# Modulation products of later layers as row sums on VectorE inside the MLPs, in place of TensorE pieces inside the mixers

## What is computed

```
# block 1, layer l (two vectors: c and c_ctx)
mx = split(silu(c)     @ w_ada[l] + b_ada[l], 6)        # w_ada[l]: 1024 x 6144
mc = split(silu(c_ctx) @ w_ada[l] + b_ada[l], 6)
hx = rmsnorm(x) * g * (1 + mx[1]) + mx[0]               # and the same for ctx
x  = x + mx[2] * rmsnorm(token_mixers(hx, ...))         # mLSTM, Fourier, convolution
hx = rmsnorm(x) * g * (1 + mx[4]) + mx[3]
x  = x + mx[5] * rmsnorm(square(relu(hx @ w1)) @ w2)    # the MLP, 1024 -> 4096 -> 1024
# block 2, layer l (one vector: c_2)
shift, scale, gate = split(silu(c_2) @ ada_w_2[l] + ada_b_2[l], 3)   # 1024 x 3072
```

## Time and profile before

| | us |
|---|---|
| median of 3 runs (3286.33 to 3298.46) | 3289.57 |
| span of the profiled execution | 3296.2 |
| TensorE busy in it | 3061.9 (93%) |
| VectorE busy | 1369.8 (42%) |
| ScalarE busy | 1076.6 (33%) |
| GpSimd busy | 1119.3 (34%) |
| L997, 1152 records of 72 ada pieces | 101.5 |

### The profile page before, as it was taken

How to read it: one execution, slowest core, us unless ns; L and a number is a source line. 1 busy time by engine, 2 the same in 40 slices (tenths; PEclk the granted TensorE clock), 3 DMA queues, 4 the chain that set the end, 5 groups by cost and what they waited for, 6 DMA issues and landing times.

```text
span 3296.2 us, 42947 instructions
## 1 busy us (share of the span) xinstructions
PE 3061.9 (93%) x16748; PEld 2466.0 (75%) x16748; DVE 1369.8 (42%) x2601; ACT 1076.6 (33%) x1995; POOL 1119.3 (34%) x862
## 2 busy tenths in 40 slices
PE   7998879999999988978999999999889999998898
PEld 4687658888888866856788876777678767776786
DVE  4683432512122158242531125644482255434822
ACT  3223432323222242243333332233433322334332
POOL 1121104133233422203344442342355523332555
PEclk9999869899999979988899989999999899999999
DMA  5232252121111112333222222121112222121121
GB/s 205 90 141 84 100 195 77 45 64 63 60 65 64 65 59 78 112 113 109 100 96 96 91 84 77 64 69 67 58 58 77 85 71 70 65 65 64 58 77 64
DMA packets 77720, 275.49 MB, mean 84 GB/s; under 512 B 8512, under 2 KB 10304, under 8 KB 77392
## 3 DMA queue, kind: packets, MB, share of 16 engines
q1 hardware_dynamic: 75824, 268.91, 24.0%
q10 hardware_dynamic: 1696, 3.84, 0.3%
HBM read 270.62 MB, written 2.10 MB: 83 GB/s over the span
## 4 chain that ended last, share of the span: by engine, by line
PE 82%; DVE 11%; ACT 3%; issue 2%; POOL 1%; DMA 1%; SPq 0%; DVEq 0%; ACTq 0%; POOLq 0%
PE pb L1054 19%; PE pb L1056 18%; PE pb L1055 18%; PE pb L1165 2%; PE pb L997 2%; PE pb L1076 2%; PE pb L1078 2%; PE pb L1077 2%; PE pb L1093 1%; DVE AR L1717 1%; PE pb L1094 1%; PE pb L1095 1%; PE pb L1123 1%; PE pb L1173 1%; PE pb L1299 1%
## 5 line engine op out<-in xcount | busy, mean ns | idle before, releaser
L2622 POOL TENSOR_TENSOR RGR<-RG,WHI 128x512 fp32r<-128x512 f32 x708 | 933.9, 1328 | 1746.3 <-ACT WHI L2210 1745.5
L2210 ACT ACTIVATE WHI<-RG 128x512 fp32r<-128x512 f32 x708 | 436.9, 624 | 711.4 <-PE pb L1056 600.5
L1054 PE MATMUL pb<-HI,WHI 128*128 128x512 f32 (+1 forms) x880 | 374.5, 426 | 10.5 <-DVE LO L1645 4.9
L1056 PE MATMUL pb<-LO,WHI 128*128 128x512 f32 (+1 forms) x880 | 351.3, 399 | 0.0
L1055 PE MATMUL pb<-HI,RGR 128*128 128x512 f32 (+1 forms) x880 | 350.7, 398 | 0.0
L1054 PE MATMUL pb<-HR,WHI 128*128 128x512 f32 (+1 forms) x768 | 276.8, 360 | 8.1 <-DVE HR L1645 5.6
L1056 PE MATMUL pb<-HR,WHI 128*128 128x512 f32 (+1 forms) x768 | 276.9, 361 | 0.0
L1055 PE MATMUL pb<-HR,RGR 128*128 128x512 f32 (+1 forms) x768 | 276.6, 360 | 0.0
L1056 PE MATMUL pb<-HIDR,WHI 128*128 128x512 f32 (+1 forms) x768 | 274.7, 358 | 0.0
L1055 PE MATMUL pb<-HIDR,RGR 128*128 128x512 f32 (+1 forms) x768 | 274.2, 357 | 0.0
L1054 PE MATMUL pb<-HIDR,WHI 128*128 128x512 f32 (+1 forms) x768 | 273.3, 356 | 0.0
(11 more groups left out here) (407 smaller groups left out, 5665.1 us busy)
## 6 DMA issues: line engine op xcount, KB each, us to landing
RG<-in_W_dram SPq DMA_DIRECT2D x504, 512.0 KB, 3.5
XCX<-in_xT_dram ACTq DMA_DIRECT2D x4, 512.0 KB, 12.2
out_dram<-XCX SPq DMA_DIRECT2D x8, 256.0 KB, 2.1
CS<-in_CST_dram ACTq DMA_DIRECT2D x1, 1027.0 KB, 4.8
XCC<-in_ctxT_dram SPq DMA_DIRECT2D x4, 256.0 KB, 13.9
CS<-in_CST_dram SPq DMA_DIRECT2D x1, 523.0 KB, 4.7
RG<-in_W_dram SPq DMA_DIRECT2D x2, 256.0 KB, 2.9
RG<-in_W_dram SPq DMA_DIRECT2D x2, 128.0 KB, 2.6
```

The costliest lines, as they stand in the source:

```text
L1054: e.matmul(out, hi[:, k, :], xh, start=k == order[0], stop=False)
L1056: i = e.matmul(out, hi[:, k, :], xl, start=False, stop=k == order[7])
L2210: e.activation(WHI[:, u % 2, h * n:h * n + n], RG[:, s % RING, h * n:h * n + n], ACT.Copy).then_inc(*up("weightsA", (u, h)))
L2622: e.tensor_tensor(RGR[:, s % RING, sl], RG[:, s % RING, sl], WHI[:, u % 2, sl].bitcast(F32), SUB).then_inc(*up("weightsG", (u, h)))
```

## The change

In the layer-0 mixer only the first 12 ada pieces stay (output channels 16 to 39 of w_ada[0], in units of 128), in the layer-1 mixer none of its 18. The other 84 units of 128 channels are computed as "columns": the slab now holds the transposed weights of 128 output channels, one channel to a partition, with the 1024 inputs along the row. VectorE multiplies it elementwise by silu(c), spread over all partitions, and sums along the row into `MODS`; for w_ada twice, for c and c_ctx. `spread` loads the spread vectors on ScalarE's DMA queue after w_out, `spreadSilu` applies Silu, `offsets` adds the biases after the MLP. In layer 0's MLP one column follows every task from the fifth to the 52nd, in layer 1's from the fifth to the 40th; the slab of a column enters the ring between two weight slabs, and the next slab but five waits for VectorE to have summed it.

```diff
+    def next_column(self):
+        if self.loaded and (len(self.loaded) > 1 or not self.sums):
+            self.step("column", self.loaded.pop(0))
+        if self.sums:
+            self.column(*self.sums.pop(0))
...
     def filling(self, us):
...
+        elif self.credit >= self.period and (self.sums or self.loaded):
+            self.credit = 0.0
+            self.next_column()
...
     if l == 0:
-        o.fill(8.5, (0, range(16, 48, 2), "w_ada", 0), (1, range(0, 40, 2), "w_ada", 1))
-    else:
-        o.fill(24.0, (2, range(0, 24, 2), "ada_w_2", 0), (3, range(8, 20, 2), "ada_w_2", 1))
+        o.fill(8.5, (0, range(16, 40, 2), "w_ada", 0))
...
+    o.step("spread", l)
...
+    if l == 0:
+        o.columns(8.0, (0, range(40, 48), "w_ada", 0), (1, range(0, 40), "w_ada", 1))
+    else:
+        o.columns(5.0, (2, range(0, 24), "ada_w_2", 0), (3, range(8, 20), "ada_w_2", 1))
+    o.step("spreadSilu", l)
     o.products(jobs, (0, 1, 2, 3), 2)
     o.flush()
+    o.columned()
...
             if i >= RING:
-                e.wait_ge(*at("matmuls", o.slabs[i - RING]["last"]))
+                older = o.slabs[i - RING]["last"]
+                e.wait_ge(*at("columnsV" if o.pieces[older]["kind"] == "column" else "matmuls", older))
...
+        def column(n):
+            p = o.pieces[n]
+            s, i = p["slabs"][0], p["i"]
+            w = RG[:, s % RING, :]
+            e.wait_ge(*at(f"slab{s % RING}", s))
+            e.wait_ge(*at("spreadA", min(i, 2)))
+            if i < 2:
+                if ("product", i) in seen:
+                    e.wait_ge(*now("columnsV"))
+                seen.add(("product", i))
+                e.scalar_tensor_tensor(out=PRODUCT, in0=w, scalar=1.0, in1=SPREAD[0][:, 0, :], op0=MUL, op1=MUL,
+                                       accum_out=MODS[i][:, p["j"], 0:1]).then_inc(*up("columnsV"))
+                e.wait_ge(*now("columnsV"))
+                e.scalar_tensor_tensor(out=w, in0=w, scalar=1.0, in1=SPREAD[0][:, 1, :], op0=MUL, op1=MUL,
+                                       accum_out=MODS[i][:, p["j"], 1:2]).then_inc(*up("columnsV", n))
+            else:
+                w4 = w.rearrange("p (a b) -> p a b", a=4)
+                e.scalar_tensor_tensor(out=w4, in0=w4, scalar=1.0, in1=SPREAD[1], op0=MUL, op1=MUL,
+                                       accum_out=MODS[i][:, p["j"], 0:1]).then_inc(*up("columnsV", n))
```

More of the change, by code:

```diff
@@ L157, in __init__ @@
         self.fills, self.soon, self.laid, self.held = [], [], [], []
+        self.sums, self.loaded = [], []
         self.credit, self.period = 0.0, 7.0
@@ L219, in ada, with column, columns, columned @@
         self.soon.append(n)
+    def column(self, i, j, name, l):
+        n = self.piece("column", [self.slab(name + ":T", l, 0, 8, j * 128, 128)], [], [], i=i, j=j, how="column")
+        self.last["column", i] = n
+        self.loaded.append(n)
+    def columns(self, period, *what):
+        self.period, self.credit = period, 0.0
+        for i, js, name, l in what:
+            self.sums += [(i, j, name, l) for j in js]
+    def next_column(self):
[3 more added lines that the diff above has]
+            self.column(*self.sums.pop(0))
+    def columned(self):
+        while self.sums or self.loaded:
+            self.next_column()
     def hold(self, i, j, name, l):
@@ L418, in place @@
                 first.setdefault(self.pieces[what[1]].get("unit"), i)
+            if what[0] == "column":
+                taken[what[1]] = i
             if what[0] == "ev":
@@ L606, in first_layer @@
     o.filled()
-    o.step("gains", l, (1, 2, 3))
+    o.step("gains", l, (1, 2) if l == 0 else (1, 2, 3))
     tag = f"o{l}a"
@@ L623, in first_layer @@
         tab = o.begin([("table", i) for i in range(7)], 12.0)
+    if l == 0:
[3 more added lines that the diff above has]
+    o.step("spreadSilu", l)
     o.products(jobs, (0, 1, 2, 3), 2)
     o.flush()
+    o.columned()
+    if l == 0:
+        o.step("offsets", 0, 40, 48)
+        o.step("offsets", 1, 0, 40)
+        o.step("gains", 0, (3,))
+    else:
+        o.step("offsets", 2, 0, 24)
+        o.step("offsets", 3, 8, 20)
     if tab:
@@ L1577, in post, with offsets @@
                 e.tensor_tensor(d, d, raw, ADD).then_inc(*up("evacV", ("roped", n)))
+        def column(n):
[13 more added lines that the diff above has]
+                                       accum_out=MODS[i][:, p["j"], 1:2]).then_inc(*up("columnsV", n))
+            else:
+                w4 = w.rearrange("p (a b) -> p a b", a=4)
+                e.scalar_tensor_tensor(out=w4, in0=w4, scalar=1.0, in1=SPREAD[1], op0=MUL, op1=MUL,
+                                       accum_out=MODS[i][:, p["j"], 0:1]).then_inc(*up("columnsV", n))
+        def offsets(i, j0, j1):
+            ns = 2 if i < 2 else 1
+            bias = vec(*(("b_ada", i) if i < 2 else ("ada_b_2", i - 2)))
+            mod = MODS[i][:, j0:j1, 0:ns]
+            e.wait_ge(*now("columnsV"))
+            e.tensor_tensor(mod, mod, bias[:, j0:j1].unsqueeze(2).to_broadcast([128, j1 - j0, ns]), ADD).then_inc(*up("columnsV", ("all", i, j0)))
         def xsum(k):
@@ L1598, in gains @@
         def gains(l, which):
-            e.wait_ge(*at("evacV", o.last["ada", l, 0 if which == (0,) else 2]))
+            if which == (3,):
+                e.wait_ge(*at("columnsV", ("all", 0, 40)))
+            else:
+                if which == (0,) and l:
+                    e.wait_ge(*at("columnsV", ("all", 1, 0)))
+                else:
+                    e.wait_ge(*at("evacV", o.last["ada", l, 0 if which == (0,) else 2]))
             e.wait_ge(*now("normV"))
@@ L1606, in gains2 @@
         def gains2(l, i):
-            e.wait_ge(*at("evacV", o.last["ada", 2 + l, i]))
+            if l == 0:
+                e.wait_ge(*at("columnsV", ("all", 2, 0)))
+            else:
+                e.wait_ge(*at("columnsV", ("all", 3, 8)))
+                e.wait_ge(*at("evacV", o.last["ada", 3, i]))
             e.wait_ge(*now("normV"))
@@ L2210, in split, with spread, spreadSilu @@
             e.activation(WHI[:, u % 2, h * n:h * n + n], RG[:, s % RING, h * n:h * n + n], ACT.Copy).then_inc(*up("weightsA", (u, h)))
+        def spread(l):
+            e.wait_ge(*at("matmuls", o.last["out", l, "evacV", None]))
+            if l == 0:
+                e.wait_ge(*at("normG", ("heads lo", 0, CHUNKS[1][5])))
+                e.dma_start(fl(SPREAD[0]), dram["VEC"][:, NVEC:NVEC + 2 * D]).then_inc(*up("spread", l, by=16))
+            else:
+                e.dma_start(SPREAD[1], dram["VEC"][:, NVEC + 2 * D:NVEC + 3 * D].rearrange("p (a b) -> p a b", a=4)).then_inc(*up("spread", l, by=16))
+        def spreadSilu(l):
+            e.wait_ge(*at("spread", l))
+            if l == 0:
+                e.activation(SPREAD[0], SPREAD[0], ACT.Silu).then_inc(*up("spreadA", 0, 1))
+            else:
+                e.activation(SPREAD[1], SPREAD[1], ACT.Silu).then_inc(*up("spreadA", 2))
         def square(x, tag):
```

18 lines of the change are left out of this document (13 added, 5 removed).

## The result

The changed kernel takes **3370.22 us** in the median of four runs (3364.94 to 3375.49), beside 3287.95 for the kernel before: a ratio of 1.023 (95% interval 1.021 to 1.025), slower, 9 us above the forecast of 3361. Its profiled execution spans 3364.1 us, 67.9 more than before. The medians are 82 us apart: the profiled execution of the kernel before is the longest of its four (3298.46), and that of the changed kernel lies 4 us under its median, so a difference of two whole traces can be some 10 us off.

What follows compares the result with a forecast made beforehand. TensorE was taken as the bound, busy 93% of the 3296.2 us span and alone pacing the MLPs. Loss 129 us against gain 58 us made 71 us slower, 3367 us in the trace, 3361 us as median; range 3280 to 3430.

Steps and rivals of the forecast that it cites:

- The loop: MLP relu2 tasks: sum, slab loads, split ahead of Relu, next sum; 10.5 us in layer 1, 11.8 in layer 0.
- loss in the MLPs: Both MLPs: 45 us in layer 0, 78 us in layer 1 and 6 us for the clock, 129 us.
- Layer 1: 78 us predicted: Layer 1's MLP: 17 loop steps of 4.9 us, 83 us, less 5 us of slack.
- Layer 0: 45 us predicted: Layer 0's MLP: 19 loop steps of 3.4 us, 64 us, less slack of 5 + 7 + 7 us.
- the last four find enough slack: Layer 0's MLP: the last four columns were left out of the 19 counted loop steps.
- The gain: Both mixers: removing 42 TensorE pieces saves 38 us in layer 0 and 20 in layer 1; bounds 35 and 90.
- the 3 us: Layer-0 mixer, 289 to 375 us: gain added for the pieces removed there, 3 us.
- The clock: MLPs: stalls lower the clock for matmuls just after a group, 6 us for five groups.
- lower bound of the gain: Mixers: a gain of only 35 us, as with emptier mixers the clock sinks further.
- Room on VectorE is real: Rival, MLPs: the loop is cut somewhere, TensorE keeps its pace and the gain stands; 3232 us, chance 15%.
- Half-speed columns: Rival, MLPs: columns take 2.35 us each, loops lengthen, 58 us more; 3419 us, chance 5%.
- the two cancel: Rival: no contention, and most of the mixers' idle time is won; about 3290 us, chance 7%.

Runs made afterwards that it cites:

- either cut: Two runs on the changed kernel: each column summed one task sooner, 3217.86 us; or, in relu2 tasks, ScalarE's first split put behind the Relu and rounded copy, 3225.57 us.
- mixer half alone: Changed kernel without its columns: the 42 TensorE pieces removed, no column slabs loaded or summed, offsets only copying biases; 3219.09 us, ratio 0.9775.
- the five pieces back: Kernel with the pieces removed but no columns (3219.09 us), with five of its 24 removed layer-0 pieces, thirteenth to seventeenth, put back: 3244.85 us, ratio 0.9860.

## Why the prediction was right, and where it was off

**The sign and the mechanism: right.** The loop was there link by link, either cut ends it, and VectorE's work outside the ring costs nothing. The term "loss in the MLPs" was 129 us and measured 146. One of its signs was wrong: TensorE was to be idle in relu2 tasks and not in plus tasks, but 17 to 18 of its some 50 us of added idle time in each MLP lie in plus tasks. The Relus run a whole turn late by then, so the last turns of a group fall into the first plus tasks behind it, which wait for their slabs and for `HIDR`: in layer 1 the first two behind the second group (from 1764.2 us) take 13.20 and 7.18 us instead of 5.58.

**Layer 1: 78 us predicted, 71.3 measured.** 17 steps of 9.86 - 5.57 us are 73 us, so the count of steps holds, and hardly any of the 5 us of slack came off. The terms of the turn: 4.6 us for the two loads (4.7 from the issue to the split), 0.54 from the split's start to the Relu's, from the Relu's start to the sum's 3.35 us (2.7 and 0.55 were set down: the square, held by GpSimd as feared, takes 1.44 us where the earlier trace rows has 0.69), and the sum 1.22 us where 1.28 + 0.7 were. The sum is not held: it starts 0.03 us ahead of GpSimd's subtraction, and it is the subtraction that takes 2.31 us then. Hence 9.86 and not 10.5.

**Layer 0: 45 us predicted, 74.8 measured.** This is the term that was mis-sized. The sum of two was set at twice 1.28 plus 0.7 us of holding, 3.3 in all, and is 3.5 with the hand-over (740.06 to 743.5). But the turns are 12.3 and 13.2 us, not 11.8; 19 steps of 0.95 us are 18 us of the 30 that are missing. In the shorter turn the added terms are 0.36 us from the issue to the split (4.96 for 4.6) and about 0.1 each for the way from the Relu to the sum and for the sums; the longer one has, besides, two loads that took 0.8 us more than those of the other, and why they did stays open. Another 6 us were put at nothing, since "the last four find enough slack": two tasks there (from 1053.1 and 1063.2 us) take 10.07 and 12.81 us instead of 8.42. The third task, which is slow in the kernel before too, takes 1.5 us more, at a granted clock of 0.79 for 0.88. The 4 us that are left are slack that was counted and not found.

**The gain: 58 us predicted, 80 measured by the traces, 74 by the ratio of the mixer half alone.** Taken apart by one VectorE line, the heads' normalisation, which is untouched (L1922 before, L2005 after: count, ns, first and last start, one fence each), and by TensorE's timeline of the changed kernel at w_out's first matmul:

```profile
L1922 DVE SCALAR_TENSOR_TENSOR AR<-pb,VC,AR x40: 340/344/353, 369.2 to 1518.0; 128x128 f32<-128x128 f32 x40
```

```profile
L2005 DVE SCALAR_TENSOR_TENSOR AR<-pb,VC,AR x40: 341/344/352, 346.8 to 1516.8; 128x128 f32<-128x128 f32 x40
```

```profile
439.62 1.09 PE L1385 MATMUL pb<-CS,AR 128*128 128x128 f32 x4 [7.22 <-DVE AR L2005]
440.36 0.56 PE L1098 MATMUL pb<-MXH,WHI 128*128 128x256 f32 x1
```

By the medians only the gain is smaller, not the loss: the changed kernel lies 151 us above the mixer half alone, its trace 150. At the first instruction of that line, 369.2 us, the changed kernel is 22.4 us ahead; the prediction gave the pieces up to 375 us 3 us. By the last transposes (477.73 and 439.62) it is 38.1 ahead, so 15.7 more where 19 was said. By w_out (495.32 and 440.36) 55.0, so 16.9 more where 16.2 was said: the stretch ahead of w_out shrank to nothing, as named. Layer 1 gave 24.0 for 20. The term that was mis-sized is the 3 us. Those five pieces stand among full-length tasks of the products, where TensorE always has work and every piece is on the path; and the chain of waits of the kernel before shows there (289 to 375 us)

```profile
306.23 6.00 DMA RG<-in_W_dram
```

a weight slab that came late, with the slabs of the pieces in the ring ahead of it. With the five pieces back the wait is back as well (5.67 us); without them it is not among the longest pieces of the chain. That is the ring again, this time on the side of the gain. The earlier trace rows had the same wait in sum, 21.8 us, and the prediction used it only as a hint at what the MLPs would do. Against its assumption that "a removed piece often only lengthens the wait behind it", five pieces put back cost 26 us.

**The clock.** 6 us were set down for it in the MLPs, and that is about what it cost. The granted clock of the two MLPs fell from 0.99 to 0.96, but in the turns TensorE waits anyway. Where it had almost no idle time and a lower clock are three tasks of layer 1: 6.96, 7.18 and 8.76 us (from 1654.9, 1777.4 and 1877.1 us, at 0.78, 0.76 and 0.65) instead of 5.58, together 6 us and an upper bound. In the emptier mixer the clock did not sink as the lower bound of the gain supposed: 0.83 from 375 to 478 us, 0.72 before:

```profile
375.00:478.00 103.00, 70.80 (x411) 62.91 (x410) 39.77 (x139) 32.69 (x70) 25.48 (x23) 0.83 0.06 20
```

w_out's matmuls, which run at the 2.4 GHz level (0.98 from 440 to 501 us), have moved into that stretch. Up to w_out alone (353 to 440 us, and 353 to 477.7 us before) it is 0.76 for 0.72: no lower, and hardly higher.

**The rivals.** "Room on VectorE is real" was right about VectorE and wrong about the ring: one condition less in the code makes it the outcome (3218 us, forecast 3232). "Half-speed columns" fell (1.28 us was reckoned from two rows, it is 1.22), and "the two cancel" with the loop's length. The total came within 9 us by luck, because errors met, as the traces have them: 22 us more gain, 17 us more loss and 2 us elsewhere make 3 us less, and the median lies 6 us above the span where 6 below were taken.

## What to carry to other kernels

Before work is moved to an idle engine, follow its buffers: a resource that was freed by the fast engine alone (here a place in a ring of loads issued in order) is now freed by a chain of three, and the period of that chain, not the idle share of the engine, decides. Write the circle down, compare its length with the step of the bottleneck, and if it is longer, move the release one step earlier or take a wait from the front of somebody else's queue; one condition did it here. A longer ring, or the columns on a load queue of their own, was not tried. Pieces that stand where the bottleneck always has work cost their full length and what they displace from the ring.

## What the runs showed of the hardware

- A two-source VectorE instruction and GpSimd's subtraction, all sources in SBUF, did not overlap in any pair looked at here: the later one ends, to 0.15 us, where it would if it had waited for the other to finish, and its record grows by that. 8 numbers per row took 1.11 us behind a subtraction and 0.16 without; a 128x1024 sum 2.18 and 1.22; the subtraction 2.31 behind a sum and 1.26 without. The page SBUF — State Buffer of the Trainium skill (who interferes with whom) states such a lock for instructions with two SBUF inputs against a GpSimd instruction that reads SBUF; the trace agrees. In the turn shown a start 0.03 us earlier decides who waits.
- The multiply with a sum along the row takes 1.22 us for 128x1024 with both float32 sources in SBUF, and 0.08 us for a second instruction that reads the sum. The Vector Engine (DVE) Microarchitecture Reference of the Trainium skill (section 7) says that such sources halve the rate. These runs do not bear it out: 512 numbers take 748 ns with two such sources and 0.69 us in a copy with a single source (L1843), and 1024 take 1.22 us.
- 132 such instructions for the 84 columns added nothing to the time that the runs could tell while no slab hung on them (3218.86 and 3219.09 us).
- Two 512 KB loads issued 0.37 us apart into an empty queue land 3.6 and 4.5 us after their issue in the median of 80 such pairs of the changed kernel (540 to 2050 us); four in five are within 3.7 and 4.6, the slowest took 5.0 and 5.9.
